# Head outputs of the state-space branch: two heads at a slot, their products alternating

## The chip, the cores and the metric
The kernel runs on one core of a Trainium2 chip. A core has TensorE (PE; matrix products into PSUM, with weight loads shown as PEld), VectorE (DVE), ScalarE (ACT), GpSimd (POOL), and SyncE (SP), whose queue issues the transfers. The engines work through their own instruction streams and wait for each other on semaphores. The metric is the device time of one execution in microseconds, lower is better.

## The reference, cut to what matters
One layer of a hybrid decoder for 512 prompt tokens and 8 x 4 sample tokens: three token mixers (a Conformer convolution, a Mamba-2 state-space branch, a gated MLP over chunks) are merged by sigmoid gates, and a gated feed-forward part follows. The change touches the prompt part of the state-space branch, with 16 heads of 64 channels, a state of 128, and chunks of 128 tokens (four of them):

```python
a_cs = jnp.cumsum(dtr * a_neg.astype(f32).reshape(g, r), axis=2)
xdt = xr * dtr[..., None]
decay = jnp.exp(jnp.where(causal, a_t[..., :, None] - a_t[..., None, :], -jnp.inf))
cb = jnp.einsum('bcign,bcjgn->bcgij', cr, br)
mix = cb[:, :, :, None] * decay
y_diag = jnp.einsum('bcgrij,bcjgrp->bcigrp', mix, xdt)
...
y_off = jnp.einsum('bclgn,bcgrpn,bclgr->bclgrp', cr, h_in, jnp.exp(a_cs))
y = (y_diag + y_off).reshape(n, tp, h, p)[:, :t]
```

Per head and chunk this is one product for `y_diag` (the mix inside the chunk) and, from the second chunk on, one for `y_off` (from the state before the chunk).

## The kernel before, in words
The large weight products run in stages, in the order A, VU, X, G2, G0, Z, G1, WO, U1, D1, U2, D2. A stage is a row of slots. In each slot TensorE multiplies one weight block with all 544 tokens (`pe_quad`, line 375): a block of 8 x 128 rows is 48 products of 272 columns (each weight split into a high and a low part, three products, two halves of the tokens), one of 4 x 128 rows is 24. Stage G0 has four groups of four slots, numbered 0 to 15 here; even slots (the gate) have 48 products and odd slots (the convolution branch's output) 24. The weights land in `w_raw`; ScalarE makes the high part (`split_hi`, L309), GpSimd the low part (`split_lo`, L314, `w_split = w_raw - high`), for the slots of the next group. Behind an even slot ScalarE takes the sum out with a sigmoid (L786), behind an odd slot with a copy (L790). The copy starts GpSimd's merge (L617 multiplies, L619 adds into `mixed`), and behind the merge, in GpSimd's queue, stand the two splits of that pair of slots. For the last group of G0 they are those of stage Z, with two whole blocks; for the others a whole and a half one.

Small products of the state-space branch are put between the slots. TensorE's `between` function is called behind the products of each slot. In G0 it computes the head outputs of the heads spread one slot earlier (`y_head`), then spreads new heads. `HEADS_AFTER` says how many heads are spread behind each slot. The steps of a head h are:

- `spread(h)` on TensorE (L1093): the row of cumulated decays goes to all partitions, in PSUM bank h % 2.
- `diffs(h)` on VectorE (L1566): four subtractions of 128 columns, from PSUM into the tile T(4 + h % 2).
- ScalarE: an exponential over that tile (L830), then one of the PSUM bank into `c_dec` (L833).
- VectorE: the tile times `cbm` (L1586), then `c_dec` times C (L1589). Both read two operands from SBUF. For a group of two heads the order is `diffs` of both, then L1586 and L1589 of the first, then of the second.
- `y_head(h)` on TensorE: for each chunk the product of L1107, from the second chunk on also that of L1110 into the same columns. Even heads write PSUM partitions 0 to 63, odd heads 64 to 127, of the same bank, 2 or 3.
- `y_sum` on VectorE (L1574), once for two heads, which frees the bank. It stands ahead of the next group's `diffs`.

The tiles and `c_dec` have two buffers, so spread, `diffs` and exponentials of a head wait for the output of the head two before it. The last group's outputs stand behind the first slot of stage Z.

Of the kernel before, what the change touches and what calls it, by code (L numbers as in the profile page):

```python
# [23 lines left out]
D, SEQ, NB, TS = 1024, 512, 8, 4  # L24
# [5 lines left out]
HEADS, HD, STATE, SKW, XBC = 16, 64, 128, 4, 1536  # L30
# [5 lines left out]
NCH = SEQ // CH  # L36
# [11 lines left out]
RING = 8  # L48
GMLP_LOADS = 2 + NB

HEADS_AFTER = (0, 0, 0, 0, 0, 1, 1, 2, 1, 2, 1, 2, 2, 1, 2, 1)
ELEM = KD * P


# [84 lines left out]
def build(nc, ins, outs):  # L139
    ph = phases()  # L140
    order = [x[0] for x in PHASES]
    with ExitStack() as ctx:
# [5 lines left out]
        def sem(name):  # L148
            if name not in sems:
                sems[name] = ctx.enter_context(nc.semaphore(name))  # L150
            return sems[name]
# [35 lines left out]
        def carve(tensor, *shapes):  # L187

            out, o = [], 0
            for parts, *dims in shapes:  # L190
                n = int(np.prod(dims))
                v = tensor[0:parts, o:o + n]
                if len(dims) == 2:
                    v = v.rearrange("p (a b) -> p a b", a=dims[0])
                out.append(v)
                o += n
            assert o <= tensor.shape[1]
            return out
# [12 lines left out]
        h0 = [half[:, r] for half in (carve(u_flat, (P, 2, D))[0], carve(ca_flat, (P, 2, D))[0])  # L211
              for r in range(2)]
# [15 lines left out]
        def T(r, n=TOK):  # L228
            return temps[:, r, 0:n]
# [9 lines left out]
        misc = ctx.enter_context(nc.psum_tensor("misc", [P, 4, 512], F32))  # L239
# [77 lines left out]
        def head_groups():  # L317

            out, h = [], 0
            for n in HEADS_AFTER:  # L320
                out.append(range(h, h + n))
# [4 lines left out]
        def sample_groups():  # L326

            out, b = [], 0
            for n in SAMPLES_AFTER:
                out.append(range(b, b + n))  # L330
                b += n
            assert b == NB
            return out
# [581 lines left out]
        def _(pe):  # L915
# [64 lines left out]
            for k in range(KD):  # L980
                for n, (wp, xp) in enumerate(((0, 0), (0, 1), (1, 0))):
                    for bank, cols in ((2, slice(0, SEQ)), (1, slice(SEQ, TOK))):
                        mm = pe.matmul(misc[0:HEADS, bank, 0:cols.stop - cols.start], w_dt_split[:, wp, k],
                                       h_split[:, k, xp, cols],
                                       start=(k == 0 and n == 0), stop=(k == KD - 1 and n == 2))
# [78 lines left out]
            def chunk_sum(c):  # L1064

                if c == 0:
                    pe.wait_ge(sem("xdt"), 2 * NCH)
                    pe.wait_ge(sem("bnat"), NCH)
                pe.wait_ge(sem("xw"), c + 1)
                for g in range(2):  # L1070
                    b0 = 2 * (c % 2) + g
                    if c >= 2:
                        pe.wait_ge(sem("chunk_state"), 2 * (c - 2) + g + 1)
                    pe.matmul(misc[:, b0], bnat[:, c, g * STATE:(g + 1) * STATE], xw[:, c % 2, g * 512:(g + 1) * 512],
                              start=True, stop=True).then_inc(sem("chunk_sum"), 1)

            def cb_products():

                for g in range(2):
                    pe.wait_ge(sem("chunk_state"), 4 + 1 + g)  # L1080
                    for c in range(NCH):
                        cols = slice(c * CH, (c + 1) * CH)
                        mm = pe.matmul(misc[:, g, cols], xbc[:, 8 + g, cols], xbc[:, 10 + g, cols],
                                       start=True, stop=True)
                    mm.then_inc(sem("cb"), 1)

            def spread(h):

                if h == 0:
                    pe.wait_ge(sem("cbm"), 2)  # L1090
                if h >= 2:
                    pe.wait_ge(sem("a_exp"), h - 1)
                pe.matmul(misc[:, h % 2], head_of[0:48, h:h + 1].to_broadcast([48, P]), a_split[0:48, 0:SEQ],  # L1093
                          start=True, stop=True).then_inc(sem("a_spread"), 1)

            def y_head(h):

                b0, rows = 2 + (h // 2) % 2, slice((h % 2) * HD, (h % 2 + 1) * HD)
                if h == 0:
                    pe.wait_ge(sem("chunk_state"), 2 * NCH)  # L1100
                if h % 2 == 0 and h >= 4:
                    pe.wait_ge(sem("y_sum"), h // 2 - 1)
                pe.wait_ge(sem("mix_head"), h + 1)
                pe.wait_ge(sem("c_decayed"), h + 1)
                for c in range(NCH):
                    cols = slice(c * CH, (c + 1) * CH)
                    mm = pe.matmul(misc[rows, b0, cols], xdt[:, c, h * HD:(h + 1) * HD], T(4 + h % 2, SEQ)[:, cols],  # L1107
                                   start=True, stop=(c == 0))
                    if c:
                        mm = pe.matmul(misc[rows, b0, cols], h_chunk[:, c - 1, h * HD:(h + 1) * HD],  # L1110
                                       c_dec[:, h % 2, cols], start=False, stop=True)
                mm.then_inc(sem("y_head"), 1)

            def beside_g2(i):
                def between(s):
# [27 lines left out]
            def beside_g0(i):  # L1143
                def between(s):
                    if i == 0:
                        chunk_sum(s)
                    if (i, s) == (1, 0):
                        cb_products()
                    k = 4 * i + s
                    for h in heads[k - 1] if k else ():  # L1150
                        y_head(h)
                    for h in heads[k]:
                        spread(h)
                return between
# [5 lines left out]
            def turn_samples():  # L1160

                pe.wait_ge(sem("a_exp"), HEADS)
                pe.wait_ge(sem("y_sum"), 8)
                turn_xb(NCH)
                for g in range(2):
                    mm = pe.matmul(misc[0:SMP, 3, g * SMP:(g + 1) * SMP], xbc[:, 8 + g, SEQ:TOK],
                                   xbc[:, 10 + g, SEQ:TOK], start=True, stop=True)
                mm.then_inc(sem("cb"), 1)

            def spread_samples():  # L1170

                pe.wait_ge(sem("xdt"), 2 * NCH + 2)
                for h in range(HEADS):
                    mm = pe.matmul(misc[:, 0, h * SMP:(h + 1) * SMP], head_of[0:48, h:h + 1].to_broadcast([48, P]),
                                   a_split[0:48, SEQ:TOK], start=True, stop=True)
                mm.then_inc(sem("s_spread"), 1)

            def y_new_tokens():

                pe.wait_ge(sem("s_mix"), 1)  # L1180
                pe.wait_ge(sem("b_masked"), 1)
                for h in range(HEADS):
                    rows = slice((h % 2) * HD, (h % 2 + 1) * HD)
                    mm = pe.matmul(misc[rows, 2, 256 + (h // 2) * SMP:256 + (h // 2 + 1) * SMP], xdt_s[:, h * HD:(h + 1) * HD],
                                   temps[0:SMP, 4, h * SMP:(h + 1) * SMP], start=True, stop=True)
                mm.then_inc(sem("s_diag"), 1)
# [23 lines left out]
            def beside_z(i):  # L1210
                def between(s):
                    if (i, s) == (0, 0):
                        for h in heads[-1]:
                            y_head(h)
                    if (i, s) == (0, 1):
                        turn_samples()
                    if (i, s) == (0, 2):
                        spread_samples()
                    if (i, s) == (0, 3):
                        y_new_tokens()  # L1220
                    for b in sample_groups()[4 * i + s]:
                        sample_state(b)
                return between
# [652 lines left out]
```

## Time and profile before
| | before |
|---|---|
| runs | 1173.69, 1174.37, 1174.45 us (median 1174.37) |
| span of the profiled execution | 1173.1 us |
| TensorE busy, weight loads busy | 91%, 88% |
| VectorE, ScalarE, GpSimd busy | 52%, 34%, 50% |
| TensorE's share of the chain that ended last | 74% |
| stage G0 with the head outputs | about 377 to 492 us |

The profile is one execution. A row of the timeline gives start, duration (us), engine, line, operation, destination and sources, forms and count; a bracket at its end is idle time of the engine just before it and what ended it. Rows of one line that follow each other are merged, and the duration then runs from the first start to the last end; products are pipelined, so neighbouring rows overlap.

### The profile page before, as it was taken

How to read it: one execution, taken by the hardware profiler on the slowest of the kernel's cores; microseconds unless marked ns; L12 is line 12 of the kernel's file. 1: busy time of each engine (PE TensorE's matmuls, PEld its weight loads, DVE VectorE, ACT ScalarE, POOL GpSimd, SP SyncE). 2: the span in 40 equal slices, each digit the busy share in tenths (PEclk: the TensorE clock that was granted, in tenths of full speed). 3: DMA queues.
4: the chain of work that ended last, by engine and by line, in shares of the span. 5: the costliest groups of instructions: out<-in, count | busy, mean ns of one | idle time of the engine just before them, and what ended most of it. 6: DMA issues, size and time to landing. Idle time of an engine off the chain costs nothing.

```text
span 1173.1 us, 19914 instructions
## 1 busy us (share of the span) xinstructions
PE 1061.9 (91%) x8110; PEld 1035.6 (88%) x8110; DVE 605.3 (52%) x855; ACT 394.4 (34%) x600; POOL 588.1 (50%) x369
## 2 busy tenths in 40 slices
PE   5993399777899999999899989899999999999996
PEld 5993399656799889888899989799999999999996
DVE  5059819996844566777630235744444002444354
ACT  5332046343345255441132321343333113333210
POOL 3569977670345544534345664444443335444341
PEclk9997599898899999998699989999999999999998
DMA  7420134401112232133222432222312233231221
GB/s 228 127 73 1 36 111 83 52 10 57 55 60 82 59 106 98 56 108 130 103 93 88 149 106 79 66 73 72 105 65 73 85 103 109 72 107 56 57 75 76
DMA packets 42460, 97.92 MB, mean 83 GB/s; under 512 B 14496, under 2 KB 15392, under 8 KB 42400
## 3 DMA queue, kind: packets, MB, share of 16 engines
q1 hardware_dynamic: 42400, 97.08, 27.5%
q8 instruction: 43, 0.70, 0.2%
q14 instruction: 17, 0.14, 0.0%
HBM read 89.13 MB, written 7.93 MB: 83 GB/s over the span
## 4 chain that ended last, share of the span: by engine, by line
PE 74%; DVE 14%; POOL 7%; ACT 3%; issue 1%; DMA 0%; SPq 0%; DVEq 0%; ACTq 0%; POOLq 0%
PE accs L375 67%; POOL temps L546 4%; DVE ca L1341 3%; DVE temps L1357 2%; POOL w_split L314 1%; PE misc L1107 1%; PE misc L941 1%; PE misc L1110 1%; DVE temps L1375 1%; PE misc L934 1%; DVE temps L1600 1%; DVE branch L1705 1%; DVE temps L1376 1%; PE misc L928 1%; ACT w_split L309 1%
## 5 line engine op out<-in xcount | busy, mean ns | idle before, releaser
L375 PE MATMUL accs<-h_split,w_split 128*128 128x272 f32 x4992 | 652.2, 293 | 56.3 <-POOL w_split L314 39.0
L375 PEld LDWEIGHTS accs<-h_split,w_split 128*128 128x128 f32 x4992 | 645.3, 193 | 62.0 <-issue 54.2
L314 POOL TENSOR_TENSOR w_split<-w_raw,w_split 128x1024 fp32r<-128x1024 f32 (+3 forms) x168 | 381.9, 2284 | 244.5 <-ACT w_split L309 244.5
L375 PE MATMUL accs<-branch,w_split 128*128 128x272 f32 x2208 | 293.2, 294 | 7.8 <-DVE branch L1705 3.6
L375 PEld LDWEIGHTS accs<-branch,w_split 128*128 128x128 f32 x2208 | 286.6, 192 | 12.5 <-DVE branch L1705 4.6
L309 ACT ACTIVATE w_split<-w_raw 128x1024 fp32r<-128x1024 f32 (+3 forms) x168 | 160.4, 964 | 190.6 <-PE accs L375 190.6
L1341 DVE SCALAR_TENSOR_TENSOR ca<-part,params,ca 128x512 f32<-128x512 f32 (+1 forms) x210 | 118.4, 622 | 0.0
L617 POOL TENSOR_TENSOR temps<-temps 128x544 f32<-128x544 f32 x16 | 22.1, 1381 | 86.0 <-ACT temps L790 86.0
L730 ACT ACTIVATE temps<-accs 128x272 f32<-128x272 f32 (+2 forms) x102 | 25.4, 322 | 113.1 <-PE accs L375 100.7
L1758 DVE TENSOR_TENSOR xbc<-accs,xbc 128x544 f32<-128x544 f32 x16 | 11.6, 725 | 95.8 <-PE accs L375 95.8
L1705 DVE TENSOR_TENSOR branch<-mixed,branch 128x544 fp32r<-128x544 f32 x8 | 16.3, 2102 | 80.9 <-ACT branch L869 80.9
L1749 DVE TENSOR_TENSOR branch<-temps,branch 128x544 f32 x22 | 44.0, 1998 | 22.4 <-ACT branch L898 22.4
L1357 DVE SCALAR_TENSOR_TENSOR temps<-temps,params 128x568 f32<-128x568 f32 x36 | 39.0, 1082 | 32.1 <-ACT temps L754 32.1
L546 POOL COPY temps<-hist_x 128x24 f32<-128x24 f32 x12 | 55.3, 4615 | 0.0
L615 POOL TENSOR_TENSOR mixed<-temps 128x544 f32 (+1 forms) x8 | 11.2, 1405 | 75.2 <-ACT temps L790 75.2
L1735 DVE TENSOR_SCALAR temps<-temps,params 128x560 f32<-128x560 f32 x22 | 11.4, 520 | 71.9 <-ACT temps L730 71.9
L1746 DVE TENSOR_TENSOR temps<-accs,temps 128x272 f32<-128x272 f32 (+2 forms) x66 | 18.8, 340 | 54.6 <-PE accs L375 54.6
L585 POOL TENSOR_TENSOR ca<-ca,part 128x512 f32<-128x512 f32 x30 | 45.2, 1508 | 3.0
L786 ACT ACTIVATE temps<-accs,params 128x544 f32<-128x544 f32 x24 | 17.1, 714 | 82.7 <-PE accs L375 82.6
L552 POOL COPY tail_f<-temps 128x2 f32 (+1 forms) x22 | 4.1, 185 | 74.6 <-ACT temps L730 74.6
L1738 DVE SCALAR_TENSOR_TENSOR temps<-temps,params 128x560 f32<-128x560 f32 x44 | 37.6, 854 | 6.5 <-DVE temps L1735 1.7
L790 ACT ACTIVATE temps<-accs 128x544 f32<-128x544 f32 x24 | 14.9, 622 | 61.2 <-PE accs L375 61.1
(225 smaller groups left out, 855.3 us busy)
## 6 DMA issues: line engine op xcount, KB each, us to landing
w_raw<-in_ffn_w_up SPq DMA_DIRECT2D x44, 512.0 KB, 3.5
w_raw<-in_w_in_main SPq DMA_DIRECT2D x28, 512.0 KB, 3.6
w_raw<-in_w_gate SPq DMA_DIRECT2D x24, 512.0 KB, 3.5
w_raw<-in_ffn_w_down SPq DMA_DIRECT2D x16, 384.0 KB, 3.0
w_raw<-in_ffn_w_down SPq DMA_DIRECT2D x16, 320.0 KB, 2.8
xbc<-in_x SPq DMA_DIRECT2D x16, 272.0 KB, 5.2
w_raw<-in_w_in_z SPq DMA_DIRECT2D x8, 512.0 KB, 3.5
w_raw<-in_ssm_w_out SPq DMA_DIRECT2D x8, 512.0 KB, 3.7
```

The costliest lines, as they stand in the source:

```text
L309: act.activation(w_split[:, s, 0, 0:n], w_raw[:, s, 0:n], ACT.Copy).then_inc(w_hi[s], 1)
L314: pool.tensor_tensor(w_split[:, s, 1, 0:n], w_raw[:, s, 0:n], w_split[:, s, 0, 0:n].bitcast(F32), ALU.subtract).then_inc(w_lo[s], 1)
L375: mm = pe.matmul(accs[:, a, half, 0:HALF], w_split[:, s, wp, k * P:(k + 1) * P], rhs(s, k, xp, half), start=(first and k == 0 and n == 0), ...
L546: pool.tensor_copy(samples(temps[:, par], k - 1 + SEQ, k)[:, :, 0:k - 1], pick(hist, f)).then_inc(done, 1)
L585: pool.tensor_tensor(ca[:, CONF_SHARED, 0:SEQ], ca[:, CONF_SHARED, 0:SEQ], tap_ring[:, t % RING], ALU.add).then_inc(sem("tap_added"), 1)
L617: pool.tensor_tensor(T(2), T(r), T(2), ALU.mult).then_inc(sem("gated"), 1)
L730: ins_ = act.activation(dst, src, ACT.Copy)
L1341: ins_ = dve.scalar_tensor_tensor(out=dst, in0=src, scalar=w, in1=dst, op0=ALU.mult, op1=ALU.add)
L1357: dve.scalar_tensor_tensor(out=cv, in0=src, scalar=w, in1=cv, op0=ALU.mult, op1=ALU.add)\
L1705: dve.tensor_tensor(branch[:, mixed_at(j)[1]], mixed[:, j], branch[:, mixed_at(j)[0]].bitcast(F32), ALU.subtract).then_inc(sem("mx_lo"), 1)
L1738: dve.scalar_tensor_tensor(out=cv, in0=src, scalar=w, in1=cv, op0=ALU.mult, op1=ALU.add)\
L1749: dve.tensor_tensor(pick(branch, i * 2 + (12 + r)), prod, pick(branch, i * 2 + r).bitcast(F32), ALU.subtract).then_inc(sem("f_lo"), 1)
```

## The change
`y_head(h)` becomes `y_pair(h0)`: it waits once for both heads h0 and h0 + 1, and for each chunk issues the L1107 product of the even head, that of the odd head, then the L1110 products of both in the same order. `HEADS_AFTER` takes 0 or 2 heads at a slot, behind slots 5, 7, 9, 10, 11, 13, 14 and 15, where it had one or two behind each slot from 5 to 15. The products themselves are the same.

```diff
-HEADS_AFTER = (0, 0, 0, 0, 0, 1, 1, 2, 1, 2, 1, 2, 2, 1, 2, 1)
+HEADS_AFTER = (0, 0, 0, 0, 0, 2, 0, 2, 0, 2, 2, 2, 0, 2, 2, 2)
...
-            def y_head(h):
+            def y_pair(h0):
 
-                b0, rows = 2 + (h // 2) % 2, slice((h % 2) * HD, (h % 2 + 1) * HD)
-                if h == 0:
+                b0, pair = 2 + (h0 // 2) % 2, (h0, h0 + 1)
+                if h0 == 0:
                     pe.wait_ge(sem("chunk_state"), 2 * NCH)
-                if h % 2 == 0 and h >= 4:
-                    pe.wait_ge(sem("y_sum"), h // 2 - 1)
-                pe.wait_ge(sem("mix_head"), h + 1)
-                pe.wait_ge(sem("c_decayed"), h + 1)
+                if h0 >= 4:
+                    pe.wait_ge(sem("y_sum"), h0 // 2 - 1)
+                pe.wait_ge(sem("mix_head"), h0 + 2)
+                pe.wait_ge(sem("c_decayed"), h0 + 2)
                 for c in range(NCH):
                     cols = slice(c * CH, (c + 1) * CH)
-                    mm = pe.matmul(misc[rows, b0, cols], xdt[:, c, h * HD:(h + 1) * HD], T(4 + h % 2, SEQ)[:, cols],
-                                   start=True, stop=(c == 0))
+                    for h in pair:
+                        rows = slice((h % 2) * HD, (h % 2 + 1) * HD)
+                        mm = pe.matmul(misc[rows, b0, cols], xdt[:, c, h * HD:(h + 1) * HD],
+                                       T(4 + h % 2, SEQ)[:, cols], start=True, stop=(c == 0))
                     if c:
-                        mm = pe.matmul(misc[rows, b0, cols], h_chunk[:, c - 1, h * HD:(h + 1) * HD],
-                                       c_dec[:, h % 2, cols], start=False, stop=True)
-                mm.then_inc(sem("y_head"), 1)
+                        for h in pair:
+                            rows = slice((h % 2) * HD, (h % 2 + 1) * HD)
+                            mm = pe.matmul(misc[rows, b0, cols], h_chunk[:, c - 1, h * HD:(h + 1) * HD],
+                                           c_dec[:, h % 2, cols], start=False, stop=True)
+                            if c == NCH - 1:
+                                mm.then_inc(sem("y_head"), 1)
...
                     for h in heads[k - 1] if k else ():
-                        y_head(h)
+                        if h % 2 == 0:
+                            y_pair(h)
```

The call behind the first slot of stage Z is changed in the same way.

## Rows read from the trace of the kernel before

**Rows 1.** The page: busy time of TensorE, and the chain that ended last.

```profile
PE 1061.9 (91%) x8110; PEld 1035.6 (88%) x8110; DVE 605.3 (52%) x855; ACT 394.4 (34%) x600; POOL 588.1 (50%) x369
...
PE 74%; DVE 14%; POOL 7%; ACT 3%; issue 1%; DMA 0%; SPq 0%; DVEq 0%; ACTq 0%; POOLq 0%
```

**Rows 2.** TensorE's waits ahead of L1107: released by, us, times.

```profile
  DVE ca L1589: 1.2, 3
```

**Rows 3.** Timeline of TensorE in G0 and the first slots of Z.

```profile
421.62 0.62 PE L1107 MATMUL misc<-temps,part 128*64 128x128 f32 x4 [0.57 <-DVE ca L1589]
...
423.69 3.29 PE L375 MATMUL accs<-branch,w_split 128*128 128x272 f32 x24
427.07 0.62 PE L1107 MATMUL misc<-temps,part 128*64 128x128 f32 x4
...
428.71 0.72 PE L1093 MATMUL misc<-a_split,head_of 48*128 48x512 f32 x2
429.37 6.29 PE L375 MATMUL accs<-h_split,w_split 128*128 128x272 f32 x48
435.59 0.65 PE L1107 MATMUL misc<-temps,part 128*64 128x128 f32 x4
...
436.95 0.27 PE L1110 MATMUL misc<-ca,part 128*64 128x128 f32 x1
437.01 0.27 PE L1107 MATMUL misc<-temps,part 128*64 128x128 f32 x1
...
438.41 0.50 PE L1093 MATMUL misc<-a_split,head_of 48*128 48x512 f32 x1
438.84 3.29 PE L375 MATMUL accs<-branch,w_split 128*128 128x272 f32 x24
...
499.68 6.29 PE L375 MATMUL accs<-h_split,w_split 128*128 128x272 f32 x48
```

**Rows 4.** Timeline of ScalarE: the copies behind slots 5, 7, 13 and 15.

```profile
414.44 0.62 ACT L790 ACTIVATE temps<-accs 128x544 f32<-128x544 f32 x1 [3.15 <-PE accs L375]
...
427.02 0.62 ACT L790 ACTIVATE temps<-accs 128x544 f32<-128x544 f32 x1 [0.94 <-PE accs L375]
...
472.91 0.62 ACT L790 ACTIVATE temps<-accs 128x544 f32<-128x544 f32 x1
...
488.36 0.62 ACT L790 ACTIVATE temps<-accs 128x544 f32<-128x544 f32 x1
```

**Rows 5.** Timeline of VectorE: head 0, head 3 and head 11.

```profile
417.56 1.10 DVE L1586 TENSOR_TENSOR temps<-temps,ca 128x512 f32<-128x512 f32 x1 [1.50 <-ACT temps L830]
418.59 2.88 DVE L1589 TENSOR_TENSOR ca<-ca,xbc 128x512 f32<-128x512 f32 x1
...
435.80 0.68 DVE L1589 TENSOR_TENSOR ca<-ca,xbc 128x512 f32<-128x512 f32 x1
...
473.58 0.69 DVE L1589 TENSOR_TENSOR ca<-ca,xbc 128x512 f32<-128x512 f32 x1
```

**Rows 6.** Timeline of GpSimd behind slots 5 and 13; the first split of slot 5.

```profile
416.75 1.37 POOL L619 TENSOR_TENSOR mixed<-mixed,temps 128x544 f32 x1 [0.19 <-POOL temps L617]
418.07 2.85 POOL L314 TENSOR_TENSOR w_split<-w_raw,w_split 128x1024 fp32r<-128x1024 f32 x1
...
418.07 4.54 POOL L314 TENSOR_TENSOR w_split<-w_raw,w_split 128x1024 fp32r<-128x1024 f32 x2
...
476.83 5.21 POOL L314 TENSOR_TENSOR w_split<-w_raw,w_split 128x1024 fp32r<-128x1024 f32 x2
```

**Rows 7.** Stretches (busy, granted clock, DMA), then the chain of waits in Z.

```profile
438.00:450.00 12.00, 11.69 (x88) 10.54 (x86) 8.46 (x17) 6.35 (x10) 6.74 (x4) 1.00 0.37 136
...
527.00:530.00 3.00, 3.00 (x14) 2.91 (x13) 2.96 (x2) 0.00 (x0) 3.00 (x2) 0.50 0.02 3
```

```profile
522.70 1.89 issue
...
527.29 7.35 PE accs L375 x48
...
582.68 8.51 PE accs L375 x48
```

More of the change, by code:

```diff
@@ L1213, in between @@
                         for h in heads[-1]:
-                            y_head(h)
+                            if h % 2 == 0:
+                                y_pair(h)
                     if (i, s) == (0, 1):
```

## The prediction

> **What bounds the kernel now.** I read the page first: TensorE is busy 91% of the span and carries 74% of the chain that ended last [rows 1]. The reader is to see that anything taken off TensorE counts, unless TensorE then waits. Next I read TensorE's order of time in stage G0, where all edits lie. The stage has 16 slots, numbered 0 to 15; a slot is one weight block times all tokens. An even slot has 48 products (6.22 us: from 429.37 to the head products at 435.59), an odd one 24 [rows 3]. Behind each slot stand, in program order, the head outputs of the heads spread one slot earlier, then the spreads of new heads. Last I read VectorE and GpSimd in the same stretch, because they decide when a head is ready.
>
> The head products are 128x64 weights against 128 columns. One head has seven products (four of L1107, three of L1110), and two instructions stand for each: 14. One head alone takes 428.71 - 427.07 = 1.64 us; two heads one after the other take 438.41 - 435.59 = 2.82 us, not 3.28 [rows 3]. The missing part is the interesting one: where head 2 ends and head 3 begins, instructions of both start in turn 55 ns apart (436.95, 437.01), against 109 ns inside one head. So two heads, which write different halves of the output partitions, do run side by side when the sequence allows it.
>
> **Part 1, the products alternate.** Two heads side by side need 14 steps of 0.109 us and the same 0.12 us of ends as a single head: 1.70 us (estimate; bounds: 1.64, a head alone, and 2.82, a pair now). I take 1.70, since the row at the border shows two halves each at its full pace. Before, there are five pairs and six single heads (heads 0, 1, 4, 7, 12, 15): 5 x 2.82 + 6 x 1.64 = 23.9 us. After, eight pairs: 13.6 us. Spreads: a single one with its changeover costs 0.43 us (438.41 to 438.84), two 0.66 us (428.71 to 429.37) [rows 3]; 6 x 0.43 + 5 x 0.66 = 5.9 becomes 8 x 0.66 = 5.3. TensorE's own work falls by 10.3 + 0.6 = 10.9 us.
>
> The Trainium skill, page "TensorE: Matmul & The Clock Gate", section "The mechanism" in Part 3, says that a weight load overlaps running products only where the row groups differ. All these products use the same 128 rows and differ in columns alone. By that rule a pair would cost two heads in full; the sum by it is rival C. The rows at 436.95 and 437.01 speak against it.
>
> **Part 2, two heads at a slot.** Here the gain goes. A pair may start only when both heads are ready; before, the first head of a pair started without the second. What makes them ready is a chain: spread, subtraction on VectorE, exponentials on ScalarE, then four products on VectorE, in the order L1586, L1589 of the first head, L1586, L1589 of the second. I count from A, the start of ScalarE's copy (L790) behind an odd slot: 414.44 in slot 5, 427.02 in slot 7, 472.91 in slot 13, 488.36 in slot 15 [rows 4]. That copy also starts GpSimd: L617, L619, then the weight splits L314. GpSimd and VectorE take turns in whole instructions. In slot 5, L619 ends at 418.12 and L1586 ends 0.54 later, at 418.66; the first L314 (418.07 + 2.85) then ends at 420.92, and L1589, which takes 0.69 us when alone, takes 2.88 and ends 0.55 behind it, at 421.47 [rows 5, 6].
>
> So for a pair spread behind an odd slot the end is pinned by GpSimd, whenever the spread came. Slot 7 shows it: the second head's L1589 ends at 436.48, A + 9.46, though a head output stood ahead of its spreads [rows 4, 5]. For slot 5 with a pair I work it out: GpSimd ends at 422.61 (418.07 + 4.54) [rows 6], the second head's two operations follow (0.55 + 0.61 + 0.08), and the pair starts 0.15 us later (as 421.47 is followed by the first product at 421.62 today [rows 3]): 424.0, A + 9.55. Today this end is hidden: behind an odd slot stand a head output (1.64), spreads (0.66) and the even slot (6.22), and the first head of the pair needs no second. After the change, slots 5, 7, 9 and 13 have only spreads there: TensorE comes to the pair at A - 0.11 + 0.66 + 6.23 = A + 6.78 and waits 2.8 us. In slot 13 the second split is a whole block for stage Z, not half a one; that pair of splits takes 5.21 us [rows 6] where slot 5's takes 4.54. With the whole block in place of half (1.15 us more) the pair starts at A + 10.7, a wait of 3.9 us.
>
> A pair spread behind an even slot meets no GpSimd work but a short slot: today's slot 12 to 13 gives L1589 of the second head ending at 474.27, A + 1.36 [rows 4, 5], so the pair starts at A + 1.5, a wait of 1.5 us in slots 11 and 15.
>
> Now the sum, from A to A of the odd slots. From the start of an odd slot to its A are 3.33 us (423.69 to 427.02).
> - 5 to 7 and 7 to 9: 9.55 + 1.70 + 3.33 = 14.58 each.
> - 9 to 11: 9.55 + 1.70 + 0.66 + 3.33 = 15.24.
> - 11 to 13: pair at 1.5, spreads at 3.2, even slot done at 10.1, when heads 8 and 9 are just ready (their splits are delayed by the turns, about 10.0); 10.1 + 1.70 + 3.33 = 15.1.
> - 13 to 15: 10.7 + 1.70 + 0.66 + 3.33 = 16.4.
> - 15 to the second slot of Z: the last pair at 11.2 (10.0 and 1.15 for the whole block), then 1.70: 12.9.
>
> Together 88.8 us. Before, from 414.44 to 499.68 [rows 3, 4], 85.2 us. At full clock the change costs 3.6 us: 10.9 us less work, and 16.4 us of waits (3 x 2.8 + 3.9 + 2 x 1.5 + 1.1) where before has about 2, 1.2 of it named as VectorE's [rows 2].
>
> **Part 3, TensorE's clock.** The middle of G0 now runs at a granted clock of 1.00, the upper level of 2.4 GHz [rows 7]. In stage Z the first wait of 1.89 us amid small products is followed by a stretch at 0.50, which is 1.2 GHz; four 48-product slots of Z follow such waits, the first takes 7.35 us, the last 8.51, in place of 6.22 [rows 7]. That is 1.13 to 2.29 us each, 1.71 in the middle. Four waits of 2.8 to 3.9 us are new, each longer than that one. 4 x 1.71 = 6.8 us; bounds 0 (no drop, since the work around these waits is dense, unlike Z's) and 6 x 2.29 with the two 1.5 us waits, 14 us. I take 6.8, the middle, since the waits are longer but the work beside them is denser than in Z.
>
> Nothing else moves. SP's queue waits for head outputs only to load states, and the weight splits come a slot or more ahead of use. Behind the last pair, Z starts from the same relation between the engines as now.
>
> **Sum against the run.** The profiled span is 1173.1 us, the median 1174.37, 1.3 us more around the same work. 3.6 + 6.8 = 10.4; 1174.4 + 10.4 = 1184.8.
>
> **The rivals.**
> A, waits but no clock loss: 1174.4 + 3.6 = 1178. For it: the waits stand amid dense work, and the clock stays at 1.00 in the middle of G0 across its short waits. Against: Z's rows. Chance 0.15.
> B, faster: the second head's operations slip between GpSimd's. If VectorE's L1586 and L1589 for the second head ran unhindered beside GpSimd, the four would start at 417.56, A + 3.1, and follow each other at 0.61 us: both heads ready by A + 5.6, before TensorE comes at A + 6.78. The 10.9 us of work would then be gain almost whole, less the 3 us in slots 11 and 15: 1174.4 - 8 = 1166. It decides from the point where the chain ends before A + 6.8. Against it: L1589 at 2.88 us in slot 5, and the end at A + 9.46 in slot 7 [rows 4, 5]. Chance 0.08. Something between A and B, within 0.2%: 0.07.
> C, the halves do not run side by side in this order: a pair costs 2 x 1.64 = 3.28 us in place of 1.70, on the path eight times: 8 x 1.58 = 12.6 more, 1191 at full clock and 1197 with the clock term. Chance 0.05.
> The forecast itself: 0.65.
>
> **Range and chances.** The range goes from 1176.5 (A with a microsecond of luck in the turns) to 1191 (3.6 with a clock term of 13, just inside its upper bound). About 0.2% (2.3 us) is what a measurement of this kernel can tell from no change. Slower 0.65 + 0.15 + 0.05 = 0.85, same 0.07, faster 0.08.
>
> **What the changed profile would show.** L1107 and L1110 starting 55 ns apart over a whole pair, and 1.7 us from its first to the next spread: part 1 right; 3 us: rival C. TensorE idle before L1107, released by L1589, 2.8 us three times, 3.9 once, 1.5 twice: part 2 right. If these are below 1 us, the turns with GpSimd are wrong and B holds. A granted clock of 0.50 in stretches between 424 and 500 us, and slots of 48 products above 7 us: part 3 right; 1.00 throughout: A. The prediction would be wrong at its root if GpSimd's L314 ended clearly earlier than A + 8.

## The result, and the profile after

| | before | changed |
|---|---|---|
| median | 1174.2 us (4 runs) | 1185.6 us (4 runs, 1183.3 to 1188.3) |
| ratio | | 1.0092 (1.008 to 1.0104) |
| span of the profiled execution | 1173.1 us | 1182.2 us |
| copy behind slot 5 to the second slot of Z | 85.2 us | 95.2 us |
| second slot of Z to the end of the span | 673.4 us | 673.0 us |

The change costs 9.1 us between the two profiled executions, 11.4 us between the medians. The four runs of the changed kernel lie in two pairs, 1183.3 and 1184.0, then 1187.2 and 1188.3 us; the median falls between them, where no run is, and the profiled execution is of the lower pair. The last two rows say where: from 414.01 to 509.21 us the changed kernel takes 10.0 us more, and nothing more behind it. In the changed file the head products stand on L1109 and L1114 (before: L1107 and L1110), the two products of VectorE on L1593 and L1596 (L1586 and L1589), the subtractions on L1573. One of the twelve runs of e5 below took 1226.4 us at a mean granted clock of 0.81 and is left out; all others count.

TensorE's timeline of the changed kernel answers to [rows 3]. It shows the pair behind slot 6, its short slot, then the same for slot 8, and the pair and the short slot behind slot 14:

```profile
413.91 0.72 PE L1093 MATMUL misc<-a_split,head_of 48*128 48x512 f32 x2
414.56 6.29 PE L375 MATMUL accs<-h_split,w_split 128*128 128x272 f32 x48
423.48 0.80 PE L1109 MATMUL misc<-temps,part 128*64 128x128 f32 x8 [2.62 <-DVE ca L1596]
...
426.34 3.70 PE L375 MATMUL accs<-branch,w_split 128*128 128x272 f32 x24
...
439.53 0.66 PE L1109 MATMUL misc<-temps,part 128*64 128x128 f32 x8 [2.61 <-DVE ca L1596]
439.99 0.42 PE L1114 MATMUL misc<-ca,part 128*64 128x128 f32 x4
440.21 0.42 PE L1109 MATMUL misc<-temps,part 128*64 128x128 f32 x4
440.43 0.42 PE L1114 MATMUL misc<-ca,part 128*64 128x128 f32 x4
...
441.21 3.27 PE L375 MATMUL accs<-branch,w_split 128*128 128x272 f32 x24
...
487.91 0.66 PE L1109 MATMUL misc<-temps,part 128*64 128x128 f32 x8 [3.74 <-DVE ca L1596]
...
491.52 5.08 PE L375 MATMUL accs<-branch,w_split 128*128 128x272 f32 x24
```

Two things are to be seen. The pair at 439.53 is done in 1.68 us (to 441.21): four instructions start in 0.22 us, 55 ns each, over the whole pair. And ahead of the pairs that were spread behind slots 5, 7, 9 and 13 TensorE stands still: 2.62, 2.61, 2.62 and 3.74 us. These are called the four long waits below. Two more, of 1.10 us behind slot 12 and 2.39 us behind the first slot of Z, belong to the pairs spread behind slots 11 and 15. All waits ahead of L1109 (us in all, how many, the longest), against 1.2 us in [rows 2]:

```profile
PE misc L1109 <- DVE ca L1596: 15.1, 6, 3.7
```

VectorE and GpSimd behind slot 5 answer to [rows 5, 6]. The copy (A) starts at 414.01.

```profile
417.14 1.11 DVE L1593 TENSOR_TENSOR temps<-temps,ca 128x512 f32<-128x512 f32 x1 [0.47 <-ACT temps L830]
418.18 2.88 DVE L1596 TENSOR_TENSOR ca<-ca,xbc 128x512 f32<-128x512 f32 x1
420.98 1.75 DVE L1593 TENSOR_TENSOR temps<-temps,ca 128x512 f32<-128x512 f32 x1
422.66 0.68 DVE L1596 TENSOR_TENSOR ca<-ca,xbc 128x512 f32<-128x512 f32 x1
```

```profile
416.34 1.37 POOL L619 TENSOR_TENSOR mixed<-mixed,temps 128x544 f32 x1 [0.19 <-POOL temps L617]
417.66 4.53 POOL L314 TENSOR_TENSOR w_split<-w_raw,w_split 128x1024 fp32r<-128x1024 f32 x2
```

Four operations that take 0.68 us each when alone (2.5 us in a row) last from 417.14 to 423.34. GpSimd's second split ends at 422.19, the second head's last operation 1.15 us later, at A + 9.33.

The third thing is the clock. Stretches of the changed kernel in us, with TensorE's, its weight loads', VectorE's, ScalarE's and GpSimd's busy time, the granted clock, DMA share and GB/s:

```profile
424.00:428.00 4.00, 4.00 (x33) 3.67 (x31) 0.75 (x1) 0.00 (x0) 0.00 (x0) 0.59 0.20 60
428.00:454.00 26.00, 20.77 (x171) 19.20 (x169) 17.44 (x25) 15.91 (x21) 14.41 (x8) 1.00 0.34 110
454.00:462.00 8.00, 8.00 (x50) 7.02 (x51) 5.26 (x13) 2.51 (x5) 0.00 (x0) 0.57 0.23 69
462.00:489.00 27.00, 22.16 (x204) 20.41 (x204) 17.58 (x27) 15.44 (x20) 14.61 (x8) 0.99 0.25 79
489.00:496.00 7.00, 7.00 (x37) 6.02 (x34) 5.28 (x13) 2.15 (x4) 0.00 (x0) 0.53 0.00 1
...
414.00:509.00 95.00, 79.92 (x647) 72.89 (x648) 63.71 (x103) 50.09 (x68) 44.94 (x25) 0.91 0.25 78
```

In the kernel before the mean of this stretch was 1.00:

```profile
414.00:500.00 86.00, 84.47 (x654) 77.20 (x653) 57.88 (x104) 49.39 (x68) 43.59 (x24) 1.00 0.27 86
```

Now 1.2 GHz is granted for a time behind three of the four long waits, and the slots of 24 products behind these pairs take 3.70, 4.89 and 5.08 us in place of 3.3; the pairs and spreads beside them are slower too.

### The profile page after: what moved, and what is told of

Same layout as the page of the kernel before. It is cut to its first block, busy times and chain, and to the rows that moved or that the text cites. A ratio compares the mean times of both kernels' runs of the same rounds, so it can differ in the third digit from the quotient of the medians.

```text
span 1182.2 us, 19906 instructions
## 1 busy us (share of the span) xinstructions
PE 1056.3 (89%) x8110; PEld 1030.4 (87%) x8110; DVE 609.6 (52%) x855; ACT 394.3 (33%) x600; POOL 588.9 (50%) x369
## 4 chain that ended last, share of the span: by engine, by line
PE 71%; DVE 16%; POOL 7%; ACT 4%; issue 1%; DMA 0%; SPq 0%; DVEq 0%; ACTq 0%; POOLq 0%
PE accs L375 65%; POOL temps L546 4%; DVE ca L1348 3%; DVE temps L1364 2%; DVE ca L1596 2%; DVE temps L1593 1%; POOL w_split L314 1%; PE misc L1109 1%; PE misc L934 1%; DVE temps L1382 1%; PE misc L941 1%; ACT w_split L309 1%; DVE temps L1607 1%; PE misc L928 1%; DVE branch L1712 1%
## 5 line engine op out<-in xcount | busy, mean ns | idle before, releaser
L1765 DVE TENSOR_TENSOR xbc<-accs,xbc 128x544 f32<-128x544 f32 x16 | 11.6, 725 | 95.9 <-PE accs L375 95.9
L1742 DVE TENSOR_SCALAR temps<-temps,params 128x560 f32<-128x560 f32 x22 | 11.4, 520 | 71.8 <-ACT temps L730 71.8
```

## The experiments

The theory on trial has three parts: the alternation halves a pair; the common wait for both heads stands on TensorE's path, because GpSimd's splits hold back VectorE's products; the long waits cost clock on top. In the table, "stage" is the time from the copy behind slot 5 to the start of the second slot of Z in the profiled execution, "rest" what lies behind it. Ratios are to the kernel before on the same chip.

| kernel | median us | ratio (interval) | stage us | rest us |
|---|---|---|---|---|
| before | 1174.2 | 1 | 85.2 | 673.4 |
| changed | 1185.6 | 1.0092 (1.008 to 1.0104) | 95.2 | 673.0 |
| changed again (e8) | 1185.0 | 1.0083 (1.007 to 1.0096) | 94.0 | 676.9 |
| e1, head after head | 1191.4 | 1.0139 (1.0122 to 1.0156) | 102.4 | 673.3 |
| e2, filled waits | 1180.2 | 1.0032 (1.0018 to 1.0046) | 88.1 | 676.6 |
| e3, short splits | 1165.2 | 0.9917 (0.9901 to 0.9934) | 75.3 | 675.2 |
| e4, split first | 1169.0 | 0.9948 (0.9935 to 0.996) | 78.4 | 675.4 |
| e10, e4 again | 1168.3 | 0.9947 (0.9933 to 0.9961) | 78.4 | 673.4 |
| e5, split first in before | 1176.5 | 1.0003 (0.9991 to 1.0015) | 84.6 | 676.7 |
| e6, schedule alone | 1180.2 | 1.0041 (1.0028 to 1.0054) | 89.2 | 675.5 |
| e7, products alone | 1174.2 | 0.9991 (0.9981 to 1.0001) | 85.0 | 673.0 |
| e9, both splits aside | 1179.9 | 1.0044 (1.003 to 1.0058) | 89.9 | 674.9 |

### Part 1 undone: head after head

```diff
-                for c in range(NCH):
-                    cols = slice(c * CH, (c + 1) * CH)
-                    for h in pair:
-                        rows = slice((h % 2) * HD, (h % 2 + 1) * HD)
+                for h in pair:
+                    rows = slice((h % 2) * HD, (h % 2 + 1) * HD)
+                    for c in range(NCH):
+                        cols = slice(c * CH, (c + 1) * CH)
...
```

> The changed kernel with the seven products of the even head issued ahead of the seven of the odd head; one common wait ahead of both, same schedule. If the alternation is what makes two heads run side by side, each of the eight pairs takes 2.8 us again in place of 1.7, and all eight stand on TensorE's path: 8 x 1.1 = 9 us above the changed kernel, near 1194.5. If the engine overlaps two neighbouring heads equally well in either order, it stays at 1185.6, and part 1 of the change brings nothing.

At full clock the pair went back to 2.79 us (468.17 to 471.62, less 0.66 for the spreads), against 1.68 in the changed kernel. TensorE's timeline of e1, slots 11 to 12:

```profile
468.17 0.62 PE L1109 MATMUL misc<-temps,part 128*64 128x128 f32 x4 [1.54 <-DVE ca L1593]
471.62 6.29 PE L375 MATMUL accs<-h_split,w_split 128*128 128x272 f32 x48
```

The whole rose by 1191.4 - 1185.0 = 6.4 us over e8, the changed kernel once more, and not by 9; its stage was 7.2 and 8.4 us longer than in the two profiles of the changed kernel. Part of the miss is the clock: in e1 the stretch at 1.2 GHz behind a wait covers the longer head products, and the slots of 24 products behind them keep their 3.3 us. Behind the first wait, pair and slot together take 1.2 us more than in the changed kernel (431.49 - 423.84 = 7.7 against 429.97 - 423.48 = 6.5), behind the second, where the changed kernel kept its clock, 2.8 us more. The alternation is real, worth 1.1 us a pair, and "no effect of the order" is out.

### Part 1 alone: the products without the schedule

```diff
...
-                    for h in heads[k - 1] if k else ():
-                        y_head(h)
+                    ready = heads[k - 1] if k else ()
+                    if len(ready) == 2 and ready[0] % 2 == 0:
+                        y_pair(ready[0])
+                    else:
+                        for h in ready:
+                            y_head(h)
```

> The kernel before with its own schedule (one or two heads at a slot); only where the two heads of a slot are an even and the next odd one (heads 2 and 3, 8 and 9, 10 and 11) they are computed alternating, behind one common wait for both. If a pair's end is set by the readiness of its second head, the shorter products only replace time in which the first head ran alone: within 0.5 us of before, 1174. If products removed from TensorE count, three pairs save 1.1 us each: 1171.

Measured: 1174.2 us, ratio 0.9991, stage 85.0 against 85.2. Three pairs got 1.1 us shorter each and started about that much later. TensorE's timeline of e7, the pair of heads 2 and 3:

```profile
435.51 0.66 PE L1127 MATMUL misc<-temps,part 128*64 128x128 f32 x8 [0.96 <-DVE ca L1616]
437.62 3.29 PE L375 MATMUL accs<-branch,w_split 128*128 128x272 f32 x24
```

The pair's end is set by its second head. Before, the first head's products ran in the time in which the second was not ready; that time is now a wait of 0.96 us (0.97 and 1.55 us for the two other pairs).

### Part 2 alone: the schedule without the alternation

The edit is the new line `HEADS_AFTER` in the kernel before.

> The kernel before with the new HEADS_AFTER alone: two heads at the same slots as in the changed kernel, but computed one after the other, each behind a wait of its own. The first head starts at A + 7.2, the second at A + 9.5, so the pair ends as late as the alternating one does (A + 11.1), but the long wait falls into two of 0.4 and some 0.8 us. If the clock falls because of the length of one wait, it stays at 1.00 here, and the time is that of the waits alone, about 3 above before: 1177 to 1178. If it falls because of the schedule as such, the time is that of the changed kernel, 1185.

Measured: 1180.2 us, ratio 1.0041; the stage took 89.2 us (4.0 more than before; 3 were expected) at a clock of 1.00. The last 2 us of the median lie in the rest of the kernel (675.5 against 673.4); the kernel before ran at 1175.3 on this chip. The clock of e6, then TensorE's timeline: heads 2 and 3, and head 10:

```profile
414.00:503.00 89.00, 83.07 (x649) 76.44 (x648) 61.08 (x103) 49.50 (x68) 44.66 (x24) 1.00 0.27 84
```

```profile
435.65 0.62 PE L1107 MATMUL misc<-temps,part 128*64 128x128 f32 x4 [0.34 <-DVE ca L1589]
437.93 0.62 PE L1107 MATMUL misc<-temps,part 128*64 128x128 f32 x4 [0.57 <-DVE ca L1589]
...
483.54 0.62 PE L1107 MATMUL misc<-temps,part 128*64 128x128 f32 x4 [2.54 <-DVE ca L1589]
```

The wait of 2.6 us became 0.34 and 0.57 us with a head between them. So the schedule costs 4 us by itself. e1 has the same schedule and the same order of products, only with one wait for both heads in place of one each: its clock fell behind all four long waits, and its stage is 102.4 us against 89.2. The common wait, then, is what lets the clock fall. But one wait of 2.54 us stayed here without a fall of the clock; a length of 2.5 us is not a sure sign.

### The clock: filling the waits with work

```diff
+                for _ in range({0: 11, 2: 11, 4: 11, 10: 16}.get(h0, 0)):
+                    pe.matmul(misc[:, b0, 0:P], ones, ident, start=True, stop=True)
                 pe.wait_ge(sem("mix_head"), h0 + 2)
```

> The changed kernel with extra products ahead of the waits of the pairs 0, 2, 4 (11 products of 128 columns, about 2.4 us) and 10 (16, about 3.5 us), into PSUM columns that the pair writes afterwards; their results are not used. TensorE is then busy through the four long waits. If the clock loss behind the waits is real, the granted clock stays at 1.00 through this stage, the slots of 24 products behind the pairs go back to 3.2 us, and the time falls by about 7 to 1178, although more is computed. If the whole loss is waiting alone, the time stays at 1185.6 or rises by the part of the filling that sticks out.

Measured: 1180.2 us, 5 us below the changed kernel, although TensorE computes 49 products, 98 instructions, more. Its clock and waits:

```profile
414.00:503.00 89.00, 84.30 (x753) 78.06 (x753) 61.15 (x104) 49.74 (x68) 44.71 (x24) 1.00 0.26 84
```

```profile
438.60 0.66 PE L1111 MATMUL misc<-temps,part 128*64 128x128 f32 x8 [0.17 <-DVE ca L1598]
440.28 3.29 PE L375 MATMUL accs<-branch,w_split 128*128 128x272 f32 x24
```

The pair starts as late as in the changed kernel (A + 9.47), but all slots of 24 products take 3.3 us. The stage is 88.1 us: the waits, less the work that was saved, cost 88.1 - 85.2 = 2.9 us, the clock 95.2 - 88.1 = 7.1 us (5.9 from e8's profile, 94.0 us). At full clock, then, the alternating pairs bring the stage 1.1 us below e6's 89.2, which has the same schedule without them. The total came out 2 us above the 1178 expected. Its ten runs fall into two groups, 1175.7 to 1176.7 (four) and 1180.2 to 1181.5 (six); the profiled one is of the upper, and its excess lies behind the stage (676.6 against 673.0 us), where nothing was edited.

### The cause of the waits: shorter splits on GpSimd

```diff
...
-                pool_phase(name, work)
+                pool_phase(name, work, 64 if n0 == 8 else None)
```

The number is the columns that `split_lo` covers; most of the low parts stay stale, so this kernel leaves work out and is no candidate.

> Leaves out a part: the GpSimd splits made during stage G0 (L314, for the next group's weights) cover 64 columns in place of 512 or 1024, so the low parts of those weights are mostly stale. All waits and the order stay. If GpSimd's splits hold back VectorE's products of the second head, both heads of a pair behind an odd slot are ready at A + 6.0 (A: the start of the copy behind the slot), TensorE does not wait in slots 6, 8, 10 and 14, the clock stays at 1.00, and the stage from slot 5's A to the second slot of Z takes 75.4 us in place of 95.2: near 1165. If the chain is long by VectorE's or ScalarE's own work, the waits stay at 2.6 us and the time above 1178.

Measured: 1165.2 us, stage 75.3 us (75.4 expected), clock 1.00. The second head behind slot 5 is ready at A + 6.30 (6.0 expected, 9.33 in the changed kernel). No wait ahead of a pair is left but the two behind even slots:

```profile
PE misc L1109 <- DVE ca L1596: 3.1, 2, 1.6
```

With the same instructions in the same order on VectorE and ScalarE the long waits went. GpSimd's splits were their cause.

### The order of GpSimd: split first

```diff
                     for r in range(2):
+                        if early:
+                            split_lo(pool, ahead[0], ahead[1], 2 * r)
                         work(i, r)
                         if ahead is not None:
-                            split_lo(pool, ahead[0], ahead[1], 2 * r)
+                            if not early:
+                                split_lo(pool, ahead[0], ahead[1], 2 * r)
...
```

`early` is set for stage G0.

> The changed kernel with one step of GpSimd moved in stage G0: the split of the even slot's next block stands ahead of the merge of its pair of slots, not behind it, so that it runs during the short odd slot; behind the merge only the other split is left. Same work in all. By the theory of the turns a pair behind an odd slot is then ready at A + 7.2 in place of A + 9.4 (one split of 1.15 us in the way in place of 2.3 and 1.15), TensorE comes at A + 6.8 and waits 0.5 us; the last group 1.6 us. No wait is over 1.6 us, the clock stays at 1.00, the stretch from slot 5's A to the second slot of Z takes 78.7 us in place of 95.2, and the time is near 1168, below both kernels. If the waits come from elsewhere, it stays at 1185.

Measured: 1169.0 us, and 1168.3 in e10, the same kernel again (ratios 0.9948 and 0.9947): it leaves nothing out and is faster than both kernels. The stage is 78.4 us (78.7 expected), clock 1.00. TensorE, VectorE and GpSimd of e4 behind slot 5, where the copy starts at 413.39:

```profile
416.51 1.11 DVE L1596 TENSOR_TENSOR temps<-temps,ca 128x512 f32<-128x512 f32 x1 [0.47 <-ACT temps L833]
...
417.03 1.74 POOL L314 TENSOR_TENSOR w_split<-w_raw,w_split 128x512 fp32r<-128x512 f32 x1
...
417.54 1.78 DVE L1599 TENSOR_TENSOR ca<-ca,xbc 128x512 f32<-128x512 f32 x1
...
419.85 0.68 DVE L1599 TENSOR_TENSOR ca<-ca,xbc 128x512 f32<-128x512 f32 x1
...
420.67 0.66 PE L1112 MATMUL misc<-temps,part 128*64 128x128 f32 x8 [0.43 <-DVE ca L1599]
```

One half split is left in the way in place of a whole and a half; the second head is ready at A + 7.14 in place of A + 9.33, and the wait is 0.43 us.

> The kernel before with the same move of the GpSimd split. TensorE waits for heads some 2 us in all there, so at most 1 to 2 us can come back: 1173. If it gained as much as the changed kernel does from the move, the gain of that one would be the move's own and not that of the pairs.

The same move in the kernel before: ratio 1.0003, stage 84.6 us. The 1 to 2 us that were held possible did not come back: the stage is 0.6 us shorter, and the runs show no difference. So the gain of e4 is that of the pairs, set free, not of the move by itself.

> The changed kernel as it is, on the same chip as these three, for their comparison: 1185, with three or four drops of the clock between 420 and 510 us, whichever way they fall.

1185.0 us; in its profile the clock fell behind the first, second and fourth long wait, where the first profile has the first, third and fourth.

### Further: both splits aside

```diff
...
+                left = None
+                for i in range(p.quads):
+                    q, j = (p, i + 1) if i + 1 < p.quads else after(p)
+                    for r in range(2):
+                        split_lo(pool, q, j, 2 * r)
+                        if left is not None:
+                            split_lo(pool, *left)
+                        work(i, r)
+                        left = (q, j, 2 * r + 1)
+                split_lo(pool, *left)
```

> The changed kernel with both GpSimd splits of a pair of slots out of the way in stage G0: the even slot's split ahead of the merge as in e4, and the odd slot's behind the next even slot, ahead of the next merge. No split then stands between the merge and VectorE's products behind an odd slot: both heads are ready at A + 6.2, before TensorE comes at A + 6.8. Against e4 the three waits of 0.43 us and the one of 1.58 us go, 2.9 us in all; only the two waits behind even slots, 1.5 us each, stay. The stretch from slot 5's A to the second slot of Z takes 75.5 us where e4's takes 78.4, and the time is near 1166. If the postponed split now meets VectorE's products of the pairs spread behind even slots, these get longer by up to 1.2 us each and half of that is lost.

> e4 once more, on the same chip as e9, for their comparison: 0.995 of the kernel before.

The expectation for e9 fell: 1179.9 us, 11.6 above e10. Behind odd slots it did what was said, no wait is left there. Behind the even slots 10 and 14 the pairs wait 4.6 and 7.9 us in place of 1.5, and the clock falls behind both: in this stage it is 0.91 on the mean, where e4's was 1.00. Of the 14.4 us that the stage is above the 75.5 expected, 9.4 are these waits; the other 5, by difference, are the clock's.

```profile
PE misc L1121 <- DVE ca L1608: 12.5, 2, 7.9
```

```profile
479.80 2.56 DVE L1605 TENSOR_TENSOR temps<-temps,ca 128x512 f32<-128x512 f32 x1
482.29 1.81 DVE L1608 TENSOR_TENSOR ca<-ca,xbc 128x512 f32<-128x512 f32 x1
484.02 1.81 DVE L1605 TENSOR_TENSOR temps<-temps,ca 128x512 f32<-128x512 f32 x1
485.76 2.82 DVE L1608 TENSOR_TENSOR ca<-ca,xbc 128x512 f32<-128x512 f32 x1
```

```profile
477.09 4.72 POOL L314 TENSOR_TENSOR w_split<-w_raw,w_split 128x1024 fp32r<-128x1024 f32 x2 [5.05 <-ACT w_split L309]
481.77 1.77 POOL L617 TENSOR_TENSOR temps<-temps 128x544 f32<-128x544 f32 x1
483.63 1.66 POOL L619 TENSOR_TENSOR mixed<-mixed,temps 128x544 f32<-128x544 f32 x1
485.25 2.78 POOL L314 TENSOR_TENSOR w_split<-w_raw,w_split 128x1024 fp32r<-128x1024 f32 x1
```

I had priced the meeting at one operation's length, 1.2 us. The rows, behind slot 14, show that all four operations of VectorE then wait behind one of GpSimd each (behind slot 10 it is three of the four): the delay of the first pushes the others into the merge of the next slot and its split.

## Why the prediction was right

1184.8 us was forecast and 1185.6 measured. The mechanism held in parts 1 and 2; of part 3 the direction and the sum held, not the number, the size and the place of the falls. So some of the closeness is luck: in the clock term, and in a median that lies between two pairs of runs some 4 us apart. The stage was forecast at 88.8 + 6.8 = 95.6 us; the two profiles have 95.2 and 94.0. The terms of the sum, one by one:

- **Part 1.** 1.70 us a pair was taken, the rows show 1.68 at full clock. (The terms given, 14 x 0.109 + 0.12, add up to 1.65; the slip is 0.4 us over eight pairs.) The other reading, head after head, is e1's 2.79 us. The page "TensorE: Matmul & The Clock Gate" of the Trainium skill, section "The mechanism" in Part 3, lets weight loads overlap only between different row groups; by it rival C would have held. Here the halves differ in columns alone and ran side by side, so the measurement decides against that sentence.
- **The waits.** Forecast three of 2.8, one of 3.9, then 1.5 twice and 1.1. Measured 2.62, 2.61, 2.62 and 3.74, then 1.10 in slot 12 and 2.39 behind the first slot of Z. The two of 1.5 us behind slots 11 and 15 were not there in this profile: TensorE ran these slots mostly at 1.2 GHz (0.57 and 0.53 in the stretches above) and came late. e2, at full clock, has both, 1.54 us each, none behind slot 12 and 0.90 behind the first slot of Z, as forecast (1.5 twice, 0, 1.1). The 1.10 us behind slot 12 and the 2.39 us behind the first slot of Z in the changed kernel are the other side of this: without the wait in the odd slot TensorE reaches the next pair early. For the whole block in slot 13 the sum took 1.15 us, for which it shows no row; the wait there is 3.74 against 2.62 us, 1.12 more.
- **The stage at full clock.** 88.8 us forecast, 88.1 in e2.
- **The clock.** 6.8 us forecast as four falls of 1.71 us. Measured 7.1 us (95.2 - 88.1), but as three falls. From A to A against e2, slots 5 to 7 lost 1.6 us (16.07 against 14.48), 9 to 11 lost 3.1 (18.19 against 15.13), 13 to 15 lost 3.0 (19.30 against 16.26); 0.4 us came back between 11 and 13. In e8 the three cost 5.9 us (94.0 - 88.1). So four falls were taken where three came, and 1.71 us for one where the mean is 2.0 to 2.4; the near hit of the sum is partly luck. The price had been read off slots of 48 products, and the sign named for part 3, such slots above 7 us, did not come either: all in the stage take 6.29 us. What got longer are the pairs, the spreads and the slots of 24 products right behind the waits.
- **The mechanism of part 2.** The pair's start at A + 9.55 was worked out from the order of turns in slot 5; it came at 423.48, A + 9.47. e3 and e4 show the cause: with less of GpSimd in the way the second head is ready at A + 6.30 and A + 7.14, where the same counting of turns had put 6.0 and 7.2. The Trainium skill says on the page "SBUF — State Buffer", section "SBUF: two separate sides", that VectorE and GpSimd share a pair of ports under an exclusive lock: when VectorE reads two SBUF operands and GpSimd's instruction reads SBUF too, the one that starts first holds it for its whole instruction. The rows agree: operations of 0.68 us last 1.75 and 2.88 us and end 0.5 to 0.6 us behind GpSimd's.
- **Rival A** (1178, waits without clock loss) is near what e2 makes of the kernel: 2.9 us in the stage, 1176 in its lower group of runs, 1180.2 in the median. **Rival B** (1166, no waits) is near e3's condition: 1165.2. Both were priced near what was measured, and neither holds for the changed kernel.

That nothing moves behind the last pair fits the last row of the first table (673.4 and 673.0 us), within the 3 us by which this part differs between profiles of one kernel (e8: 676.9).

## What to carry to other kernels

Work taken off the busiest engine is gain only if what it waits for next is ready earlier too: find the end of that chain in the profile before, and count from there; here slots 7, 9 and 11 of the kernel before had it at A + 9.46, 9.45 and 9.46 with a head output ahead of their spreads, and the changed kernel without one at A + 9.33. Joining two waits into one for the later of both costs the time in which the first part ran alone, and a longer gap on TensorE can take its clock along. When VectorE works on two SBUF operands beside GpSimd, count whole instructions in turns, and look for a place in GpSimd's queue where its long ones meet no one: this one move turned +0.8% into -0.5%.

## What the runs showed of the hardware

- Products into the two column halves of the array (outputs on partitions 0 to 63 and 64 to 127) over the same 128 rows run side by side: a new instruction every 55 ns against 109 ns in one half, 1.68 us for 28 against 2.79 us head after head.
- A wait of 2.6 us between dense work took the clock down to 1.2 GHz in some cases and not in others: of the four long waits (2.61 to 3.74 us) in each of two profiles of one kernel, three, and all four in e1's profile. The positions differ between the two profiles. Waits of 2.54 us (e6) and 2.39 us (the changed kernel, ahead of the last pair) were followed by no fall. A fall cost 1.5 to 3.1 us from A to A here.
- Behind the stage, profiled executions of all these kernels take either about 673 us or 675 to 677 us, the kernel's text being the same there (before 673.4, changed 673.0 and 676.9, e4 675.4 and 673.4). The mean granted clock of the following 110 us does not sort them: 0.88 in the changed kernel (673.0), 0.84 in e8 (676.9), but 0.84 in the kernel before too (673.4). From 200 to 300 us behind the start of the second slot of Z it is 0.91 in the six profiles at 675.2 to 676.9 and 0.92 to 0.96 in the six at 673.0 to 674.9. What decides it was not tried. It limits what one profile can say to some 3 us.

```profile
509.00:620.00 111.00, 100.00 (x728) 95.28 (x725) 71.42 (x103) 28.75 (x39) 43.06 (x23) 0.88 0.30 105
```

```profile
508.00:618.00 110.00, 98.21 (x687) 93.55 (x687) 71.30 (x103) 28.50 (x38) 38.39 (x21) 0.84 0.30 106
```

```profile
500.00:610.00 110.00, 100.19 (x708) 96.03 (x707) 72.90 (x103) 29.66 (x39) 42.12 (x23) 0.84 0.30 107
```

The first of these rows is the changed kernel's, the second e8's, the third that of the kernel before.
